# A hybrid RWKV-7 layer on one core: the scan's instructions in another order on four engines

## What is computed

```python
def step(s, inp):
    r_t, w_t, k_t, v_t, kk_t, a_t = inp
    sa = jnp.einsum('bhvk,bhk->bhv', s, kk_t)
    s = (s * w_t[:, :, None, :] - sa[..., None] * (kk_t * a_t)[:, :, None, :]
         + v_t[..., None] * k_t[:, :, None, :])
    return s, jnp.einsum('bhvk,bhk->bhv', s, r_t)
...
y = y_fwd + y_bwd      # then group norm, a bonus term, a gate, and the output projection
```

## Time and profile before

| what | value |
|---|---|
| runs | 1142.37, 1141.38, 1136.57; median 1141.38 |
| profiled execution: its own time | 1137.16 |
| its span, first to last instruction | 1135.4 |
| outside the span | 1.8 |
| the scan, 545 to 976 of the span | 431.0, of which TensorE busy 352.4, VectorE 344.1, GpSimd 253.1, ScalarE 177.5 |
| granted TensorE clock, mean | 0.964 |

### The profile page before, as it was taken

How to read it: one execution, slowest core, us unless ns; L and a number is a source line. 1 busy time by engine, 2 the same in 40 slices (tenths; PEclk the granted TensorE clock), 3 DMA queues, 4 the chain that set the end, 5 groups by cost and what they waited for, 6 DMA issues and landing times. The chain is left out here.

```text
span 1135.4 us, 30153 instructions
## 1 busy us (share of the span) xinstructions
PE 992.5 (87%) x13387; PEld 872.2 (77%) x13387; DVE 658.5 (58%) x904; ACT 398.8 (35%) x660; POOL 415.5 (37%) x374
## 2 busy tenths in 40 slices
PE   5699999999899999999278988988888888779997
PEld 3399999999687777798278888887778777447685
DVE  5430079574473112422578888888888885365532
ACT  5351111101245564421234344444434442533321
POOL 7121211111123032221356555656666663232110
PEclk9799999999899999999569999999999999989999
DMA  9613222111130332112301222121112100541131
GB/s 358 239 38 129 103 75 75 38 38 38 37 113 9 121 121 95 69 65 61 84 20 32 45 45 41 36 54 31 31 41 49 32 12 13 226 184 42 70 111 55
DMA packets 94668, 87.34 MB, mean 77 GB/s; under 512 B 61336, under 2 KB 84036, under 8 KB 93388
## 3 DMA queue, kind: packets, MB, share of 16 engines
q1 hardware_dynamic: 94540, 85.43, 23.5%
HBM read 63.83 MB, written 21.58 MB: 75 GB/s over the span
## 5 line engine op out<-in xcount | busy, mean ns | idle before, releaser
L804 PE MATMUL ps<-input_rounded,weights_rounded 128*128 128x386 f32 x768 | 268.6, 350 | 2.9 <-DVE input_rest L919 2.8
L806 PE MATMUL ps<-input_rounded,weights_rest 128*128 128x386 f32 x768 | 261.6, 341 | 0.0
L805 PE MATMUL ps<-input_rest,weights_rounded 128*128 128x386 f32 x768 | 261.3, 340 | 0.0
L1551 POOL TENSOR_TENSOR arena<-arena,lvl 128x512 f32<-128x512 f32 x108 | 138.9, 1300 | 103.5 <-ACT arena L1474 53.1
L804 PEld LDWEIGHTS ps<-input_rounded,weights_rounded 128*128 128x128 f32 x768 | 146.1, 190 | 19.2 <-issue 17.0
L508 POOL TENSOR_TENSOR weights_rest<-arena,weights_rounded 128x2048 fp32r<-128x2048 f32 x16 | 77.3, 4833 | 213.2 <-ACT weights_rounded L553 213.2
L805 PEld LDWEIGHTS ps<-input_rest,weights_rounded 128*128 128x128 f32 x768 | 146.3, 190 | 0.9 <-issue 0.6
L806 PEld LDWEIGHTS ps<-input_rounded,weights_rest 128*128 128x128 f32 x768 | 146.2, 190 | 0.0
L1300 PE MATMUL ps<-arena 64*64 64x64 f32 x2880 | 105.0, 223 | 35.9 <-issue 30.5
L1310 PE MATMUL ps<-arena 64*64 64x64 f32 x2880 | 105.0, 223 | 26.3 <-DVE arena L1667 26.3
L1300 PEld LDWEIGHTS ps<-arena 64*64 64x64 f32 x2880 | 95.4, 137 | 42.2 <-issue 39.3
(11 more groups left out here) (240 smaller groups left out, 1631.4 us busy)
## 6 DMA issues: line engine op xcount, KB each, us to landing
arena<-in_w_in SPq DMA_DIRECT2D x16, 1024.0 KB, 6.2
lora_scratch<-zc SPq DMA_DIRECT2D x16, 579.0 KB, 3.3
zc<-lora_scratch SPq DMA_DIRECT2D x72, 128.0 KB, 3.0
arena<-in_ada_w SPq DMA_DIRECT2D x7, 1024.0 KB, 7.2
mix_scratch<-zc SPq DMA_DIRECT2D x4, 1158.0 KB, 9.7
arena<-v_scratch SPq DMA_DIRECT2D x72, 64.0 KB, 2.4
out<-arena SPq DMA_DIRECT2D x9, 512.0 KB, 2.6
zc<-in_x_sample SPq DMA_DIRECT2D x4, 1024.0 KB, 8.9
```

Source lines behind the costliest of these rows:

```text
L804: pe.matmul(o, w_hi[:, k, cut], hi_of_h[:, k, cols_b], start=(k == 0), stop=False)
L805: pe.matmul(o, w_hi[:, k, cut], lo_of_h[k][:, cols_b], start=False, stop=False)
L806: last = pe.matmul(o, w_lo[:, k, cut], hi_of_h[:, k, cols_b], start=False, stop=(k == KT - 1))
L1551: pool.tensor_tensor(Um[l % 3], UT, lvl[:, l, :].unsqueeze(1).to_broadcast([P, 2 * PAIRS, C]), ALU.mult).then_inc(q_um[l], 1)
```

## The change

No instruction is added or removed in the scan and none changes its operands; the order in which they are issued is another on TensorE, ScalarE, GpSimd and VectorE. It was found by a search over orders that used durations measured in a trace.

```diff
--- before.py
+++ after.py
@@ -1396,44 +1396,42 @@
 
                 pe.wait_ge(q_init, 1)
                 first_state()
-                for step in range(N + 2):
-                    n0, n1, n2 = step, step - 1, step - 2
-                    if n2 == PC + 2:
+                for step in range(N + 4):
+                    n2, n3, n4 = step - 2, step - 3, step - 4
+                    if 0 <= n4 < N:
+                        rhs_end(n4)
+                        product(n4, 5)
+                    if n4 == PC + 2:
                         final_state()
+                    if 0 <= n4 < N:
+                        outputs_begin(n4)
+                        update(n4, 5)
+                    if 0 <= n3 < N:
+                        product(n3, 1)
+                    if 0 <= n4 < N:
+                        solve(n4)
+                    if 0 <= n3 < N:
+                        update(n3, 1)
+                        transpose_keys(n3)
+                        product(n3, 2)
+                    if 0 <= n4 < N:
+                        new_state_part(n4)
+                    if 0 <= n3 < N:
+                        update(n3, 2)
+                    if 0 <= n4 < N:
+                        outputs_end(n4)
+                    if 0 <= n3 < N:
+                        product(n3, 3)
                     if 0 <= n2 < N:
-                        outputs_begin(n2)
-                    if 0 <= n1 < N:
-                        product(n1, 2)
+                        gram(n2, 1)
+                    if 0 <= n3 < N:
+                        update(n3, 3)
                     if 0 <= n2 < N:
-                        new_state_part(n2)
-                    if 0 <= n1 < N:
-                        update(n1, 2)
-                    if 0 <= n2 < N:
-                        outputs_end(n2)
-                    if 0 <= n1 < N:
-                        product(n1, 3)
-                    if 0 <= n0 < N:
-                        gram(n0, 0)
-                    if 0 <= n1 < N:
-                        update(n1, 3)
-                    if 0 <= n0 < N:
-                        gram(n0, 1)
-                    if 0 <= n1 < N:
-                        product(n1, 4)
-                    if 0 <= n0 < N:
-                        transpose_keys(n0)
-                    if 0 <= n1 < N:
-                        update(n1, 4)
-                        rhs_begin(n1)
-                        product(n1, 5)
-                        rhs_end(n1)
-                        update(n1, 5)
-                    if 0 <= n0 < N:
-                        product(n0, 1)
-                    if 0 <= n1 < N:
-                        solve(n1)
-                    if 0 <= n0 < N:
-                        update(n0, 1)
+                        gram(n2, 0)
+                    if 0 <= n3 < N:
+                        product(n3, 4)
+                        rhs_begin(n3)
+                        update(n3, 4)
 
             @block.scalar
             def _(act):
@@ -1494,34 +1492,36 @@
                 act.wait_ge(q_init, 1)
                 act.wait_ge(q_si, 1)
                 act.activation(S[1], by_channel(3), ACT.Copy).then_inc(q_s0, 1)
-                for step in range(N + 3):
-                    n0, n1, n2, n3 = step, step - 1, step - 2, step - 3
-                    if 0 <= n3 < N:
-                        copy_y(n3, 4)
+                for step in range(N + 2):
+                    n0, n1, n2 = step, step - 1, step - 2
                     if 0 <= n2 < N:
-                        chunk_decay(n2)
-                    if 0 <= n3 < N:
-                        negate_rhs(n3)
-                        copy_y(n3, 5)
+                        keys_by_token(n2)
+                        copy_y(n2, 2)
                     if 0 <= n1 < N:
-                        inverse_decay(n1)
-                    if 0 <= n3 < N:
-                        copy_u(n3)
-                    if n3 == PC + 2:
+                        chunk_decay(n1)
+                    if 0 <= n2 < N:
+                        copy_y(n2, 3)
+                    if 0 <= n1 < N:
+                        gather_triangle(n1)
+                    if 0 <= n2 < N:
+                        negate_rhs(n2)
+                    if n2 == PC + 2:
                         act.wait_ge(q_fs, 1)
                         act.activation(S[0], by_channel(3), ACT.Copy).then_inc(q_fc, 1)
                     if 0 <= n2 < N:
-                        copy_y(n2, 1)
-                    if 0 <= n1 < N:
-                        decay(n1)
-                    if 0 <= n2 < N:
-                        keys_by_token(n2)
-                        copy_y(n2, 2)
-                        copy_y(n2, 3)
-                    if 0 <= n1 < N:
-                        gather_triangle(n1)
+                        copy_y(n2, 4)
                     if 0 <= n0 < N:
                         key_factor(n0)
+                    if 0 <= n2 < N:
+                        copy_y(n2, 5)
+                    if 0 <= n0 < N:
+                        inverse_decay(n0)
+                    if 0 <= n2 < N:
+                        copy_u(n2)
+                    if 0 <= n1 < N:
+                        copy_y(n1, 1)
+                    if 0 <= n0 < N:
+                        decay(n0)
 
             @block.gpsimd
             def _(pool):
@@ -1586,21 +1586,23 @@
 
                 for step in range(N + 4):
                     n1, n2, n3, n4 = step - 1, step - 2, step - 3, step - 4
-                    if 0 <= n4 < N:
-                        mask_level(n4, 5)
                     if 0 <= n3 < N:
-                        mask_level(n3, 0)
-                        mask_level(n3, 1)
+                        mask_level(n3, 2)
                         mask_level(n3, 3)
-                        mask_level(n3, 4)
-                        mask_level(n3, 2)
                     if 0 <= n2 < N:
                         keys_over_decay(n2)
                         bonus_keys(n2)
                     if 0 <= n4 < N:
                         decay_state(n4)
+                    if 0 <= n3 < N:
+                        mask_level(n3, 5)
+                    if 0 <= n2 < N:
+                        mask_level(n2, 0)
+                        mask_level(n2, 1)
                     if 0 <= n1 < N:
                         b_keys(n1)
+                    if 0 <= n2 < N:
+                        mask_level(n2, 4)
 
             @block.vector
             def _(dve):
@@ -1686,37 +1688,33 @@
                             dve.tensor_tensor(yc, yc, by_channel(3)[:, d], ALU.add).then_inc(q_ye, 1)
 
                 dve.wait_ge(q_init, 1)
-                for step in range(N + 3):
-                    n0, n1, n2, n3 = step, step - 1, step - 2, step - 3
-                    if 0 <= n2 < N:
-                        transpose_x(n2, 2)
-                    if 0 <= n3 < N:
-                        add_state(n3)
+                for step in range(N + 2):
+                    n0, n1, n2 = step, step - 1, step - 2
                     if 0 <= n2 < N:
                         factor(n2, 3)
                     if 0 <= n1 < N:
-                        mask(n1, 0)
+                        mask(n1, 1)
                     if 0 <= n2 < N:
                         transpose_x(n2, 3)
                     if 0 <= n1 < N:
-                        mask(n1, 1)
+                        mask(n1, 0)
                     if 0 <= n2 < N:
                         factor(n2, 4)
-                    if 0 <= n3 < N:
-                        add_outputs(n3)
+                    if 0 <= n0 < N:
+                        sum_decays(n0)
                     if 0 <= n2 < N:
                         transpose_x(n2, 4)
                     if 0 <= n1 < N:
                         begin_inverse(n1)
-                        begin_transpose(n1)
                     if 0 <= n2 < N:
                         factor(n2, 5)
+                    if 0 <= n1 < N:
+                        begin_transpose(n1)
                     if 0 <= n0 < N:
-                        sum_decays(n0)
+                        turn_decays(n0)
                     if 0 <= n1 < N:
                         factor(n1, 1)
                     if 0 <= n0 < N:
-                        turn_decays(n0)
                         keys(n0)
                     if 0 <= n1 < N:
                         transpose_x(n1, 1)
@@ -1726,6 +1724,11 @@
                         factor(n1, 2)
                     if 0 <= n0 < N:
                         queries(n0)
+                    if 0 <= n1 < N:
+                        transpose_x(n1, 2)
+                    if 0 <= n2 < N:
+                        add_state(n2)
+                        add_outputs(n2)
 
         nc.all_engine_barrier(sems_to_clear=range(sems2[0], sems2[-1] + 1))
         part2.close()
```

## The result

The changed kernel takes 1143.39 (median of 10 runs, 1142.07 to 1145.22) against 1139.10 of the kernel before (10 runs, 1135.97 to 1142.46). The ratio is 1.0038, 95% interval 1.0023 to 1.0053: 0.4% slower, which is less than the 0.5% that I called a difference. I had forecast +11.4 and got +4.3. One run of the kernel before, at 2406.58 beside e4, e10 and e11, was a slow one and is left out of their ratios.

What follows compares the result with a forecast made beforehand. TensorE waits for VectorE, which takes turns with GpSimd. 16 steps at +0.66 (+10.6), `final_state` +0.5, start and tail +0.3 make +11.4; set on 1139.4, that is 1150.8, range 1134 to 1158.

Steps and rivals of the forecast that it cites:

- level 1 to 2: From level 1's product to level 2's: forecast 4.90 instead of 5.22, a gain of 0.32.
- level 2 to 3: From level 2's product to level 3's: forecast 6.22 (late) or 5.25 (early), a loss of 0.81 in both.
- the last segment: From level 4's product to the next level 1's: forecast 7.75 instead of 7.58, a loss of 0.17.
- late steps: The eight steps of late latent chunks: period forecast at 23.26 against 22.60.
- rival A: At the first query VectorE goes first: late steps 22.75, whole +7.3, or 1146.7; chance 0.22.
- the losing order: At the first query of late steps, GpSimd's `bonus_keys` goes first: segment 6.22 instead of 5.41, loss 0.81.
- Early steps: The eight steps of early latent chunks: period forecast at 22.29 against 21.63.
- `rhs_begin` ahead of update 4: After product 4 on TensorE: takes about 1.17, so update 4 starts at 2.25 instead of 2.09.
- The scan as an unknown: `sum_decays` ahead of mask 0: taken to hold GpSimd off for the full 0.52, segment 7.75; if not, 7.37.
- `final_state`: Between product 5 and update 5, with its round trip over ScalarE: +0.5, once (bounds 0 to 1.3).
- Start and tail: Start and tail of the kernel: +0.3 (bounds -1 to +1.5).
- F: Moved instructions keep their present durations: 21.30 in place of 22.60, about 1119, faster; chance 0.15.

Runs made afterwards that it cites:

- e4: The kernel before with turn_decays moved ahead of level 1's factor, alone: 1130.53, ratio 0.9933.
- e10: The changed kernel with a VectorE copy of 96 columns from PSUM added ahead of the first query: 1150.58, ratio 1.0119.
- e11: The changed kernel with ScalarE's two triangle copies swapped and sum_decays moved between begin_transpose and turn_decays: 1133.11, ratio 0.9953.
- e1: The changed kernel with mask 3 moved back ahead of mask 4: 1135.87, ratio 0.996.
- e3: The kernel before with begin_transpose moved behind level 5's factor, alone: 1130.83, ratio 0.9913.
- e8: The changed kernel with ScalarE's two triangle copies in VectorE's order (direction 1, then 0): 1144.24, ratio 1.003.
- e9: e5's kernel with GpSimd's bonus_keys and mask 5 moved behind decay_state: 1120.32, ratio 0.9822.
- e2: The kernel before with mask 3 moved behind mask 2, alone: 1171.26, ratio 1.027.
- e7: The changed kernel with a VectorE memset of 128 columns added ahead of the first query: 1146.51, ratio 1.0055.
- e5: The kernel before with begin_transpose behind level 5's factor and turn_decays ahead of level 1's factor: 1126.94, ratio 0.9881.

## Why the prediction was wrong

*The sign and the mechanism were right.* The new order gains in level 1 to 2 and loses in level 2 to 3 and in the last segment, because VectorE and GpSimd take turns. Four of the five segments of the table came within 0.06 of the forecast, and the causes were shown one by one: by e4 for level 1 to 2, by e1 for level 2 to 3, by e3, e8 and e11 for the last.

*The step that failed* is this: "At the first query (7.02) GpSimd has started `bonus_keys` 0.05 earlier (6.97)", and with it "so GpSimd goes first here". It started 0.03 later. Counted from level 1's product, the query came at 6.95 and not at 7.02, `bonus_keys` at 6.98 and not at 6.97. Half of this 0.08 is in the factor ahead of the query: I let it start 0.04 before the end of `b_over_decay` (6.41 against 6.45), though I had read 0.08 for such a handover, and in the trace it is 0.08 (803.65 against 803.73). With 0.08 the walk gives 6.98 against 6.97, no order at all. The error was larger than the margin on which the choice between forecast and rival A rested, and eight late steps hung on it at once. The late segment from level 2 to 3 was priced at +0.81 and measured +0.28: 8 x 0.53 = 4.2 of the 6.2 by which the 16 steps were too dear. e10, which puts the query behind, gives 6.26 and 23.21, so the term for the losing order was right in size. This was rival A in kind (22.75 forecast for it, 22.63 measured; +7.3 in the whole, +4.3 measured).

*The rest* are small sizes. Early steps came to +0.52, not +0.66, and the late ones 0.1 below A: `rhs_begin` ahead of update 4 cost nothing. I had update 4 at 2.25 after product 4, and in the timeline it starts at 2.10, when the factor allows it. That put product 5 at 4.11 instead of 4.26, but mask 0 and `begin_inverse` set level 5's factor in any case, so the segment changed only by about as much as mask 0 itself ended earlier than forecast (4.27, not 4.34).

*The scan as an unknown* was placed at the right end (held off for its whole length, e8). The segment was 7.69 against 7.75 with the hold and 7.37 without. What the Trainium skill states in SBUF — State Buffer, "SBUF: two separate sides", a whole-instruction exclusion, is what the traces show, with the scan too.

*`final_state`* shows level 5's product to the next level 1's at 4.88 instead of 3.58 in its step, +1.3, where the kernel before lost 0.77 in its own (22.40 against 21.63): +0.5 net, as taken. The forecast gave no working for this +0.5, so that it fits is luck. Start and tail, taken at +0.3, are +1.0 in the two traces: the first product starts 0.4 later, chunk 0 takes 26.72 instead of 26.22, and the end behind the last chunk is 0.1 longer. With the 4.4 of the steps that makes 5.9; the medians differ by 4.3. The profiled executions differ by more (1145.22 and 1137.16), and neither stands at its kernel's median; 1.5 of their difference lies behind the scan, in code that wasn't changed.

*What fixed durations would have said* (F, 21.3 for every late step) didn't come. F had 4.32 for level 1 to 2, 5.42 for level 2 to 3 and 7.17 for the last segment; measured are 4.88, 5.69 and 7.69. The durations were read where the order of before puts them, and in the new order the two keys take 2.40 instead of 1.75 and `begin_inverse` 1.75 instead of 1.30. That the search which found the order was misled in this way is likely, but its durations are not on record.

## What to carry to other kernels

Where two engines exclude each other, an order of instructions can't be priced with fixed durations; walk the ring with the rule of who holds the turn, and treat every place where two of them start within 0.1 of each other as two cases, each with its price, not as one forecast: the chip told leads of 0.01 apart (last section), a walk does not. Test the moves of a reordering one at a time: here two gained 5 to 10 us each, and two others took it back (mask 3 some 8, the scan with the copies some 10). After that, e9 gained some 7 more by moving the helper's work (GpSimd's) into the stretch where the busy engine reads PSUM.

## What the runs showed of the hardware beyond that

When e2 and e10 made TensorE wait longer in one place, its clock fell. In e10 two of the late steps took 24.76 instead of 23.21. There, after an idle time of 1.83, a product took 1.78 instead of 1.15 and a gram 2.08 instead of 1.16:

```profile
833.28 1.78 PE L1300 MATMUL ps<-arena 64*64 64x64 f32 x32 [1.83 <-issue]
835.00 2.08 PE L1280 MATMUL ps<-arena 64*128 64x128 f32 x16
837.00 1.15 PE L1310 MATMUL ps<-arena 64*64 64x64 f32 x32
```

The windows of the same stretch:

```profile
826.00:833.00 7.00, 4.43 (x128) 4.08 (x128) 7.00 (x11) 2.10 (x4) 6.04 (x8) 1.00 0.02 5
833.00:837.00 4.00, 3.72 (x48) 3.41 (x48) 2.10 (x5) 0.90 (x3) 2.27 (x2) 0.57 0.60 129
837.00:844.00 7.00, 6.43 (x201) 6.12 (x201) 6.16 (x9) 3.03 (x6) 1.89 (x2) 1.00 0.20 41
```

The granted clock is 0.57 for these 4 us, near the lower of its two levels (1.2 of 2.4 GHz), and 1.00 on both sides; TensorE had been busy 4.43 of the 7 before. It costs 1.55 each time, and a third one of 1.5 comes behind the last step, in chunk 17. Beside the regular periods this makes up why the profiled e10 is so long; of its other runs there is no trace. In e2 the long wait is ahead of product 2: TensorE is idle there for 2.31 (1.25 in the kernel before), and in 13 of 16 steps the clock then falls. In the other late steps of e10 the segment is 6.26 too and TensorE was busy for 4.4 of the 7 before product 3 as well, but the clock held. So neither the wait nor the busy time before it decides between them; what does stays open.

Which engine goes first at a near tie can be read from the scans of all 13 traces. In them a VectorE instruction with two SBUF inputs and a GpSimd one start within 0.12 of each other 320 times. Apart from 16 cases in e7 the rule is sharp: VectorE went first in all 135 cases in which GpSimd led by 0.009 or less (or started later), and GpSimd in all 169 in which it led by 0.011 or more. In early steps of the kernel before, for one, its lead at the first query is 0.05, and GpSimd goes first. The 16 cases are the first queries behind e7's memset: they start 0.10 to 0.11 after `bonus_keys` and still go first, while at such leads without a memset (0.09 in e5, 0.10 to 0.11 in e9) VectorE waited. So the memset does change the order; whether it takes a turn itself was not settled.
